# Paged keys at three a slot, paged values only behind the projection, and the key ring as four more value buffers

## The reference, cut to what matters

```
xn   = rms_norm(x, norm1_g);  proj = xn @ w_in            # 2048 x 5128
u, h_b, h_c, h_x, q, k, v, f = split(proj)
y    = [pool_mixer(u) | h_b * conv(h_c * h_x) | attention(q, k, v, f)]
x    = x + rms_norm_by_group(y) @ w_o                      # 2048 x 2048
x    = x + (silu(conv(a) + b) * gate) @ w_down             # a, gate = rms_norm(x) @ w_up
attention, decode: for each sequence and head
  s = k_pages . q * 128**-0.5 - forget biases;  p = softmax(s over 4096 + own);  o = p @ v_pages
```

## Time and profile before

| | us |
|---|---|
| median of 3 runs (lowest, highest) | 2901.93 (2901.82, 2904.88) |
| the profiled execution's own time | 2906.3 |
| its span in the profile | 2904.4 |

### The profile page before, as it was taken

The page is one execution under the profiler, slowest core; times in us unless marked ns, Lnnn a source line. Parts: engine busy times, 40 slices in busy tenths (PEclk is TensorE's granted clock), DMA queues, the critical chain, the costliest instruction groups (busy, mean ns, idle before and its releaser), DMA issues.

```text
span 2904.4 us, 50517 instructions
## 1 busy us (share of the span) xinstructions
PE 2654.7 (91%) x19656; PEld 2329.5 (80%) x19656; DVE 1428.7 (49%) x5629; ACT 730.8 (25%) x979; POOL 156.2 (5%) x317
## 2 busy tenths in 40 slices
PE   5899899963767779998999999999999999999998
PEld 3799889851323226666999999999999999999998
DVE  4786677669776142224343434344443434343433
ACT  4332122212223241123222122222222222222221
POOL 0100000001111221200000000000000000000000
PEclk8999999986766989998999999999999999999999
DMA  6789899887999867735223322222322222332221
GB/s 237 250 285 336 311 334 349 305 303 281 356 369 371 288 208 276 267 130 179 88 90 105 98 88 88 88 88 95 105 92 88 88 88 88 99 105 88 88 88 63
DMA packets 274530, 532.92 MB, mean 183 GB/s; under 512 B 16410, under 2 KB 177787, under 8 KB 272980
## 3 DMA queue, kind: packets, MB, share of 16 engines
q1 hardware_dynamic: 214573, 361.52, 36.3%
q0 software_dynamic: 39472, 142.46, 13.5%
q10 hardware_dynamic: 20247, 25.73, 2.5%
HBM read 503.94 MB, written 24.05 MB: 182 GB/s over the span
## 4 chain that ended last, share of the span: by engine, by line
PE 77%; DMA 10%; DVE 8%; issue 2%; SPq 1%; ACT 1%; POOLq 0%; ACTq 0%; POOL 0%; DVEq 0%
PE ps L678 76%; DMA t_r<-in_cache_k 6%; DVE t_work L1746 5%; DMA t_r<-in_cache_v 2%; DMA t_wraw<-in_w_in 1%; PE ps L681 1%; DVE t_wl L1583 0%; SPq L563 0%; ACT t_wh L1196 0%; DMA t_auxW<-in_pool_w 0%; DVE t_work L1583 0%; DVE t_xl L1583 0%; DVE t_auxW L1583 0%; DMA t_wraw<-in_w_o 0%; SPq L549 0%
## 5 line engine op out<-in xcount | busy, mean ns | idle before, releaser
L678 PE MATMUL ps<-t_xh,t_wh 128*128 128x260 f32 (+1 forms) x4352 | 951.6, 294 | 19.3 <-DVE t_xl L1583 19.2
L678 PE MATMUL ps<-t_xh,t_wl 128*128 128x260 f32 (+1 forms) x4352 | 937.8, 291 | 0.0
L678 PE MATMUL ps<-t_xl,t_wh 128*128 128x260 f32 (+1 forms) x4352 | 936.6, 291 | 0.0
L1583 DVE TENSOR_TENSOR t_wl<-t_wraw,t_wh 128x1024 fp32r<-128x1024 f32 x376 | 460.0, 1224 | 897.9 <-ACT t_wh L1196 897.9
L1196 ACT ACTIVATE t_wh<-t_wraw 128x1024 fp32r<-128x1024 f32 x376 | 398.0, 1060 | 1657.9 <-PE ps L678 1657.9
L678 PEld LDWEIGHTS ps<-t_xh,t_wh 128*128 128x128 f32 x4352 | 687.8, 190 | 99.4 <-issue 65.5
L678 PEld LDWEIGHTS ps<-t_xh,t_wl 128*128 128x128 f32 x4352 | 687.8, 190 | 11.9
L678 PEld LDWEIGHTS ps<-t_xl,t_wh 128*128 128x128 f32 x4352 | 687.6, 190 | 9.1
L1746 DVE CUSTOM_DVE_ANT_0 t_work<-t_r,t_work 128x128 f32<-128x128 f32 x2048 | 454.6, 285 | 130.8 <-DMA t_r<-in_cache_k 118.9
L678 PE MATMUL ps<-t_hh,t_wh 128*128 128x260 f32 x1408 | 285.2, 284 | 3.4 <-issue 3.4
L678 PE MATMUL ps<-t_hh,t_wl 128*128 128x260 f32 x1408 | 284.3, 283 | 0.0
(11 more groups left out here) (256 smaller groups left out, 1202.4 us busy)
## 6 DMA issues: line engine op xcount, KB each, us to landing
t_r<-in_cache_k SPq DMA_DIRECT2D x256, 512.0 KB, 6.9
t_r<-in_cache_v POOLq DMA_DIRECT2D x256, 512.0 KB, 6.1
t_wraw<-in_w_up SPq DMA_DIRECT2D x44, 2048.0 KB, 8.0
t_wraw<-in_w_in SPq DMA_DIRECT2D x22, 2048.0 KB, 9.4
t_wraw<-in_w_down SPq DMA_DIRECT2D x22, 2048.0 KB, 7.8
t_wraw<-in_w_o SPq DMA_DIRECT2D x11, 2048.0 KB, 10.2
scr_proj<-t_stg ACTq DMA_DIRECT2D x40, 256.0 KB, 4.4
t_aux<-scr_proj ACTq DMA_DIRECT2D x8, 768.0 KB, 12.3
```

What stands on the lines that cost most here:

```text
L678: return pe.matmul(out, lhsT, rhs, start=start, stop=stop)
L1583: return dve.tensor_tensor(out, in0, in1, op)
```

## The change

It has three parts. (1) `page_slots`: the key pages stand three to a slot (two in a sequence's last slot), in slots 2 to 89, with K_END at 12, 23, 34, ... 89. The value pages begin in slot 81: two a slot up to 92, then four, four and two in turn up to 148, then two. That gives 226 key pages to slots 2 to 79 and 30 to slots 80 to 89; 24 value pages to slots 81 to 92, 178 to the heads, 54 behind. (2) `value_places`: value pages whose slot lies behind the last key page (slot 89) and ahead of TAIL rotate through eight buffers, the four of `vring` and the four of `kring`. (3) Pages that fall on `kring` are loaded by SyncE, in its own slot order, with a wait for k_used (all keys) at their first use and for v_used after it; the rest by GpSimd as before. SyncE waits at TAIL for the last page that lies in `kring` (page 199) before it loads the residual. TensorE's `value_page` takes the buffer from the list.

```diff
--- before.py
+++ after.py
@@ -53,22 +53,23 @@
 HSTEP = 7
 TAIL = HEAD0 + HEADS * HSTEP
 KEY0 = 2
-K_RATE = 2
 
 
 def page_slots():
     keys, values, k_end, v_end = {}, {}, [], []
-    for n in range(DEC * PAGES):
-        keys.setdefault(KEY0 + n // K_RATE, []).append(n)
-    for r in range(DEC):
-        k_end.append(KEY0 + (PAGES * (r + 1) - 1) // K_RATE)
-    at = 0
+    at, n = KEY0, 0
+    while n < DEC * PAGES:
+        take = 3 if n % PAGES else 2
+        keys[at] = list(range(n, n + take))
+        k_end += [at] * ((n + take) // PAGES - n // PAGES)
+        n += take
+        at += 1
+    at = CHUNKS + 1
     for r in range(DEC):
         at = max(at, k_end[r] + 4)
         done = 0
         while done < PAGES:
-            rate = ((2 if at % 2 == 0 else 0) if at < CHUNKS else (2 if at % 3 else 0) if at < k_end[-1] else
-                    (4 if at % 2 == 0 else 2))
+            rate = (2 if at < HEAD0 else 4 if at % 3 and at < TAIL else 2)
             take = min(rate, PAGES - done)
             if take:
                 values[at] = [r * PAGES + done + i for i in range(take)]
@@ -84,6 +85,22 @@
 SLOTS = OUT0 + OUT_CHUNKS
 LAST = V_END[-1]
 assert LAST + 4 < SLOTS
+
+
+def value_places():
+
+
+    slot_of = {n: s for s, pages in VALUES.items() for n in pages}
+    places, held, loads = [], {}, [0] * RING + [DEC * PAGES // RING] * RING
+    for n in range(DEC * PAGES):
+        b = n % (2 * RING if K_END[-1] < slot_of[n] < TAIL else RING)
+        loads[b] += 1
+        places.append((b, loads[b], held.get(b, -1)))
+        held[b] = n
+    return places, max(held.get(b, -1) for b in range(RING, 2 * RING)), loads
+
+
+V_PLACES, V_WIDE, V_LOADS = value_places()
 K_LAST = {s: r for r, s in enumerate(K_END)}
 V_LAST = {s: r for r, s in enumerate(V_END)}
 MISC = sorted({s + d for s in K_END for d in (1, 2, 4)} | {s + 1 for s in V_END})
@@ -478,11 +495,13 @@
                     pool.dma_start(dst, src).then_inc(r_stored, 16)
 
             def value_loads(pages):
+                pages = [n for n in pages if V_PLACES[n][0] < RING]
                 numbers = [pool.value_load(ptr[0:1, n:n + 1], min_val=0, max_val=N_POOL - 1) for n in pages]
                 for n, g in zip(pages, numbers):
-                    pool.wait_ge(v_used, n + 1)
-                    pool.dma_start(vring[:, n % RING, :],
-                                   v_pages[bass.ds(g, 1), :, :].rearrange("a p n -> (a p) n")).then_inc(v_loaded[n % RING], 16)
+                    b, _, held = V_PLACES[n]
+                    pool.wait_ge(v_used, held + 1 + PRIME)
+                    pool.dma_start(vring[:, b, :],
+                                   v_pages[bass.ds(g, 1), :, :].rearrange("a p n -> (a p) n")).then_inc(v_loaded[b], 16)
 
             for s in range(SLOTS):
                 value_loads(VALUES.get(s, []))
@@ -599,6 +618,7 @@
                     load_raw(R_O + m, m, w_o_v, 2 * m * P)
                 if s == TAIL:
                     sp.wait_ge(k_used, DEC * PAGES + PRIME)
+                    sp.wait_ge(v_used, V_WIDE + 1 + PRIME)
                     res = scrx.rearrange("k p t -> p k t")
                     sp.dma_start(xT[:, 0:8, 0:SEQ], res[:, 0:8, 0:SEQ]).then_inc(res_loaded, 16)
                     sp.dma_start(work[:, 4096:7168].rearrange("p (k t) -> p k t", k=6),
@@ -612,6 +632,16 @@
                 kg = [number(n) for n in kp]
                 for n, g in zip(kp, kg):
                     page(kring, k_pages, k_loaded, k_used, g, *divmod(n, PAGES))
+                vp = [n for n in VALUES.get(s, []) if V_PLACES[n][0] >= RING]
+                vg = [number(n) for n in vp]
+                for n, g in zip(vp, vg):
+                    b, _, held = V_PLACES[n]
+                    if held < 0:
+                        sp.wait_ge(k_used, DEC * PAGES + PRIME)
+                    else:
+                        sp.wait_ge(v_used, held + 1 + PRIME)
+                    sp.dma_start(kring[:, b - RING, :],
+                                 v_pages[bass.ds(g, 1), :, :].rearrange("a p n -> (a p) n")).then_inc(k_loaded[b - RING], 16)
                 n, late = divmod(s - OUT0 + 6, 4)
                 if late == 0 and 2 <= n < 8:
                     load_raw(R_O + n, n % 2, w_o_v, 2 * n * P)
@@ -818,10 +848,12 @@
                 last.then_inc(e_tail, 1)
 
             def value_page(r, p):
-                pe.wait_ge(v_loaded[p % RING], r * (16 * PAGES // RING) + 16 * (p // RING + 1))
+                b, load, _ = V_PLACES[r * PAGES + p]
+                pe.wait_ge((v_loaded + k_loaded)[b], 16 * load)
+                buf = vring[:, b, :] if b < RING else kring[:, b - RING, :]
                 for c in range(2):
                     lane = 32 * (2 * (p % 2) + c)
-                    last = mm(ps[lane:lane + HEADS, 4, :], Eb[:, r * PAGES + p, :], vring[:, p % RING, c * 512:(c + 1) * 512],
+                    last = mm(ps[lane:lane + HEADS, 4, :], Eb[:, r * PAGES + p, :], buf[:, c * 512:(c + 1) * 512],
                               p < 2, p >= PAGES - 2)
                 last.then_inc(v_used, 1)
 
@@ -1084,7 +1116,7 @@
                         pe.wait_ge(w_loaded[1], 16 * (R_O // 2 + 6))
                         sample_out_attention(8, lambda k, c: wraw[:, 1, 2048 * k + 512 * c:2048 * k + 512 * (c + 1)])
                         for i in range(RING):
-                            pe.wait_ge(v_loaded[i], 16 * (DEC * PAGES // RING + 1))
+                            pe.wait_ge(v_loaded[i], 16 * (V_LOADS[i] + 1))
                         sample_out_attention(10, lambda k, c: vring[:, 2 * k + c // 2, 512 * (c % 2):512 * (c % 2 + 1)])\
                             .then_inc(y_norm, 1)
                     if (u, kt) == (0, 5):
```

## The result

The changed kernel takes 2974.5 us (median of 4, 2971.9 to 2985.2), the kernel before 2903.4 beside it: a ratio of 1.025, interval 1.0225 to 1.0278. It is slower, by 71 us. The direction was forecast, the size was not: 2925 us, and 2974.5 lies just outside the range of 2882 to 2972.

A forecast was written before the change was run, and what follows sets the result against it. VectorE was to bound the projection instead of TensorE, with DMA nearly bounding the heads; +55 projection, +8 mixers, -29 heads, -11 behind them gave +23 us, a 2925 us median, range over the cases 2882 to 2972.

The forecast's parts named there:

- the projection: Slots up to chunk 79: VectorE becomes the bound, its work plus key waits ending chunk 79 some 55 us later.
- The wait behind a load: Projection: VectorE waits for keys queued behind each weight load, 9.5 us for the first, 2.2 for 16 others, sum 45.
- The cover: Projection: a full key ring gives VectorE four pages of work during a weight load, 1.9 us more than before.
- VectorE's own work: Projection: 6.69 us for a slot with three key pages; 531 us without any wait, against TensorE's 450.
- The clock at half behind longer stalls: Projection: TensorE's stalls at a sequence's end get longer; the half clock after them hides in its slack, costing nothing.
- Mixers: Mixer slots: VectorE bounds, three net key pages more cost 5.8 us, DMA nearly as long; +8 (0 to +20).
- Bandwidth does not set the projection: Projection: four slots carry 8.7 MB in 29 us, 300 GB/s, under the measured 325.
- its low end of +15: Projection: the lower end of its range, with no waits behind the 16 loads, slot 79 starting at 641 us.
- Heads -29: Heads: eight value buffers keep the DMA engines full, 5.6 us a slot, 314 us instead of 343; 0 to -50.
- Behind the heads -11: Output projection: 54 value pages instead of 74 at 1.05 us a pair save 11 us (-7 to -13).
- SyncE's issues and the late residual: Heads and after: added page issues in SyncE's queue and the later residual load cost nothing, about 5 us if late.
- much slower: Rival, chance 0.14: 4.5 us wait a load in the projection, heads gain nothing because TensorE paces them; +97, 2999 us.

The follow-up runs named there:

- the ring of eight: Changed kernel with the value ring lent to the keys up to slot 72, so eight buffers for keys; 2928.7 us, ratio 1.009 to the kernel before.
- half of the scoring: Changed kernel with VectorE scoring only heads 0, 2, 4 and 6 of each key page, all pages still loaded; 2901.2 us, ratio 0.999 to the kernel before.
- one half of this one alone: Kernel before with only eight buffers for values behind slot 129 and ahead of TAIL, keys two a slot; 2878.0 us, ratio 0.991.
- the other alone: Kernel before with only the keys three a slot, values in their old slots and four buffers; 2978.9 us, ratio 1.026.
- the fastest version: Kernel before with eight value buffers behind slot 129, and the 2 MB w_in and two early w_o loads in four pieces; 2857.0 us, ratio 0.985.

## Why the prediction was wrong

VectorE did become the bound of the projection, and the eight buffers did help the heads; the direction follows from that. But three terms of the sum were mis-sized: the projection was +77 instead of +55, the mixers +27 instead of +8, the heads -20 instead of -29. In the mixers part of the mechanism was wrong too.

- **The wait behind a load: this is the term that failed most, 2.2 us where it was 3.8.** The prediction took 9.5 + 16 x 2.2 = 45 us; measured are 70.6 in all, that is 9.8 for the first and a mean of 3.8 for the 16 others (up to 5.9). The cover (8.6 us) was right: from 216.3 to 224.8. What was wrong was to stay near the wait measured with an empty queue, although the text named the pages ahead of the load: two of them at 1.4 us each make the load's 8.5 us into 11.3, and 11.1 is the measured median. The load's landing to the next page was 1.3 us before (197.9 to 199.23), so cover and delay each worked out give 11.3 + 1.3 - 8.6 = 4.0; picking the nearest measured wait instead left 26 us out.
- **VectorE's own work: 520 us where it was 531.** It began slot 79 at 698 us, not at 676. From its first key page at 100.6 that is 597 us, of which 70.6 are waits for keys and 7.2 waits for ScalarE, leaving some 520, the same as in the ring of eight. So 11 us too much work hid part of the 26 us, and the 7.2 were in no term: 26 - 11 + 7 = 22. That a second error stood against the first is luck.
- **The clock at half behind longer stalls: mostly hidden.** TensorE stood idle to 624.1 us (granted clock 0.50 from 615 to 624, half of full speed), then took 8.3 us for a chunk instead of 5.8 (0.65 from 625 to 632), and had 1.00 again from 634. Most of this lay in its slack, but VectorE's next rest of weights waited for it, 1.1 us here and 7.2 us in all.
- **Mixers: +27 instead of +8, by three things.** First, the way to the first pool part took 9.1 us more, where the prediction has nothing. The load of the pool weights took 14.4 us instead of 10.0, at a DMA share of 0.98, while key pages were loading beside it (with keys two a slot the whole way took 18.8 us). And VectorE, for which a sequence had just ended, stood 10.2 us until TensorE, which had waited for that load, passed the maximum on:

```profile
701.25 14.41 DMA t_auxW<-in_pool_w
...
719.44 0.17 DVE L1800 COPY t_maxall<-ps 128x8 f32<-128x8 f32 x1 [10.16 <-PE ps L708]
```

  Second, the three groups of three slots up to the fourth pool part took 28.3, 29.0 and 26.4 us; before they took 21.0 in the mean. Three more pages are 5.8, as worked out; the rest, 3 us in all, goes with waits for keys of 3.4 and 2.8 us in the first two groups, which were left out:

```profile
746.83 0.29 DVE L1778 CUSTOM_DVE_ANT_0 t_work<-t_r,t_work 128x128 f32<-128x128 f32 x1 [2.65 <-DMA t_r<-in_cache_k]
...
749.38 0.29 DVE L1778 CUSTOM_DVE_ANT_0 t_work<-t_r,t_work 128x128 f32<-128x128 f32 x1 [0.76 <-DMA t_r<-in_cache_k]
```

  Third, the six key pages that slots 90 to 92 lost were booked as a gain of 11.5 us; only 3 came, so there VectorE was not what the slots waited for: from 810 to 847 us, up to the maximum of head 0, it was busy for 10 us of 37, TensorE for 29. Which wait set the pace there stays open.
- **Bandwidth does not set the projection: true of the changed kernel (0.84), but its floor lay close.** With half of the scoring the projection ended at +7 and with the waits nearly gone at +22. The forecast of +55 stood 48 us above that floor, its low end of +15 only 8.
- **Heads -29: it was -20** (14.4 and 5.3), at 350 GB/s from head 0 to head 7. The 5.6 us a slot were 5.5 over these 49 slots. But they had taken only 285 us before, 5.8 a slot, where the whole stage had 343 / 56 = 6.1; so more than half of the 29 was to come from the slots around them, and these gave 5.3 behind and the 3 ahead that stand with the mixers. The gain of the eight buffers is real, 80 us against four with the same pages.
- **Behind the heads -11: right, -13.** SyncE's issues and the late residual cost nothing visible: right.

Of the rivals, much slower named what took over: it was to take the forecast's place from 3.5 us a load on, and 3.8 was measured. It had the heads wrong (no gain, where 20 us came). The measured 2974.5 lies between it (2999) and the forecast (2925).

Not settled is why the heads take 270 us in the changed kernel and 277 to 282 in three versions with the same pages and buffers that reach them earlier.

## What to carry to other kernels

Where work of one engine is moved to fill another's slack, first put each engine's time a slot beside the others' for the new load: here 6.7 us of VectorE and 6.7 of the DMA engines stood against 5.8 of TensorE, and each ruled three pages out. The small ring behind a large load in one queue paid the load minus its cover again and again, a mean of 3.8 us; work both out with the transfers that will be in flight, and cut the load in pieces or deepen the ring (the waits fell from 71 us to 28 and 9). And test the parts of a change apart: one half of this one alone was worth 26 us less, the other alone 102 us more in its stage and 76 in all.

## What the runs showed of the hardware

A load of 2 MB took 8.5 us where the key ring was served at two pages a slot and no values ran, and 10.1 to 13.1 in the changed kernel. The mix of weights, in rows of 1 KB, and key pages gave 325 GB/s at a DMA share of 0.94 (half of VectorE's work), where pages with the heads' transfers gave 350 at 0.93 in the changed kernel and up to 375 at 0.99 before. TensorE, busy for 449 of 450 us, had its full clock all the while (1.00, the fastest version).
